# Reordering five steps of VectorE's hand-written queue in the second mixer of a ten-sublayer transformer kernel

## The chip, the core and the metric

The program runs on one NeuronCore of one Trainium2 chip. The metric is the device time of one execution in microseconds (us); lower is better. Several executions are timed and their median is given. A separate execution is profiled; its trace gives the start and the duration of every instruction.

## What is computed

One sequence of 256 tokens with 1024 features goes through ten sublayers, all in float32. Two blocks are chained: the first holds (FFN, mixer 1, FFN) twice, the second holds (mixer 2, FFN) twice and a last norm. The change touches mixer 2 alone, which therefore runs twice, as sublayers 6 and 8 (counted from 0).

```python
def mixer2(h):                            # h: normed x, 256 x 1024
    z = h @ w_in                          # split by columns
    y_a = pool_mixer(pool_u)              # running means of 2, 4, 8, 16 tokens, grouped 64x64 matmuls
    y_b = chunk_band_attention(q, k, v)   # 4 heads, relative bias
    y_c = dsa_attention(q, k, v, ...)     # 4 heads over selected keys:
    #   score = sum_h iw[h] * relu(iq[h] . ik);  keep the top 64 of every row;  softmax over those
    y_d = mla_attention(...)              # 4 heads, latent queries and keys
    y = concat([y_a, y_b, y_c, y_d])      # 4 groups of 256 features
    mix = y * rsqrt(mean(y*y per group) + eps) * g
    return x + gate * (mix @ w_out)
```

## The kernel before

**Work and staging.** Activations lie with features on the 128 partitions and tokens along the free axis. Every weight arrives by DMA in half units of 512 KB in an 8-slot ring. Exact float32 products are made from float32r parts: ScalarE copies a half unit to its high part WH (`hi_half`, `hi` for both halves of a unit), VectorE subtracts to get the low part WL (`lo_half`, `lo`), and TensorE does three matmuls for each 128x128 block. Activations are split in the same way (HH and HL, YH and YL).

**Order.** Each engine's queue is written out by hand and runs strictly in that order. Engines are tied together by counting semaphores: a producer's instruction adds one, and the consumer's queue stops until the count is reached. In mixer 2, attentions are numbered a0 to a0+5 (two MLA, two selected-key, two banded; even ones for the first 128 queries, odd ones for the last 128), and output tiles, 128 queries by 256 features, are numbered o0 to o0+7.

**Life of an output tile o.** TensorE makes it in PSUM bank 6 (`attend` or `pooled`). VectorE scales it into the buffer OT (`attended2`: a reciprocal of 4 columns and a 128x256 product; `pooled`: one 128x256 product); each adds one to `s_o`. ScalarE sums its squares and forms the RMS scale (`tile_scale`, adds one to `s_oss`). VectorE puts the scale on a diagonal matrix (`diagonal`, `s_od`). TensorE turns the tile with that diagonal into PSUM bank 7 for o0 to o0+5 (`turned_out`, `s_ot`). ScalarE copies the high part YH out of the bank (`tile_out`, `s_oh`), and VectorE subtracts to get the low part YL (`tile_rest`, two 128x128 instructions, `s_ol`), which also frees the bank for the next tile.

**Selection.** VectorE finds the 64 largest scores of a row in eight rounds of 8 (`largest(t, rounds)`, in each round MAX8 and then MATCH_REPLACE8), and then `selected(t)` turns the marks into an additive mask WKR and adds one to `s_sel`. TensorE needs that mask at the start of `sa_score`. `maxima2(a, t)` reduces an attention's scores to negated row maxima, for ScalarE's exponentials.

**TensorE's order around the change.** While the last input unit (`columns(n, 9, ...)`, CAK) is multiplied, between its two halves comes `beside_cak`. Its steps wait for VectorE like this:

```python
pooled(1, o0 + 3)             # wait_ge(s_o, o0 + 3): tiles o0, o0+1 and o0+2 scaled out of bank 6
turned_out(n, o0 + 1)         # wait_ge(s_od, o0 + 2); wait_ge(s_ol, o0 + 1): tile_rest(o0) done
attend(a0 + 2, 0, r0 + 4, o0 + 4, of_sa)  # wait_ge(s_apt, r0 + 4); wait_ge(s_o, o0 + 4): VectorE's pooled(1) done
sa_score(a0 + 3, 1)           # wait_ge(s_aex, a0 + 3); wait_ge(s_sel, 2 * l + 2): selected(1) done
turned_out(n, o0 + 2)         # wait_ge(s_od, o0 + 3); wait_ge(s_ol, o0 + 2): tile_rest(o0 + 1) done
```

**ScalarE's order there:** `tile_out(o0)`, `by_keys(r0 + 3)`, `tile_scale(o0 + 2)` (waits for `s_o` of o0+3), `hi(u0 + 10)` (the first output-weight unit), `tile_scale(o0 + 3)`, `tile_out(o0 + 1)`, `tile_scale(o0 + 4)`, `tile_out(o0 + 2)`, `exponents2(a0 + 3)`.

Of the kernel before, what the change touches and what calls it, by code (L numbers as in the profile page):

```python
# [87 lines left out]
def build(nc, A):  # L88
    ctx = ExitStack()
    with ctx:  # L90
# [89 lines left out]
        def vec(name, i=0, n=1):  # L180
            return VC[:, VEC[name] + i:VEC[name] + i + n]
# [9 lines left out]
        def v3(ap, a):  # L191
            return ap.rearrange("p (a s) -> p a s", a=a)
# [146 lines left out]
        def score_bank(n, b, t):  # L339
            w = 128 * (t + 1)  # L340
            return PS[:, b:b + t + 1, :].rearrange("p a s -> p (a s)").rearrange("p (h k) -> p h k", h=4)
# [32 lines left out]
        def summed2(n, r, c):  # L374

            k, k0 = (len(ROUNDS[SUBS[n][0]][i]) for i in (r, 0))
            last = (k0 * KD if r else 0) + k * c + k - 1
            if last % 8 == 7:
                return s_half, down_half(n) + last // 8 + 1
            return s_op2, 8 * MIX_AT[n] + 4 * r + c // 2 + 1  # L380
# [4 lines left out]
        def out_bank2(n, r, c):  # L385
            banks = out_banks(n, r)
            return PS[:, banks[c % len(banks)], 0:256]

        def turn_bank(n, o):

            o -= OUT0[n]
            return 6 + o % 2 if SUBS[n][0] == "mix1" else (7, 7, 7, 7, 7, 7, 4, 5)[o]
# [9 lines left out]
        def gains_of(n):  # L402
            return f"gmix{SUBS[n][1]}" if SUBS[n][0] == "mix1" else f"ggroup{SUBS[n][1]}"
# [1273 lines left out]
        def _(e):  # L1677
            count = {"step": 0}

            def step(ins):  # L1680

                count["step"] += 1
                ins.then_inc(s_dstep, 1)
                e.wait_ge(s_dstep, count["step"])

            def ts(out, a, s1, s2, op0, op1):
                return e.tensor_scalar(out, a, s1, s2, op0) if s2 is None else e.tensor_scalar(out, a, s1, s2, op0, op1)  # L1687

            def tt(out, a, b, op):
                return e.tensor_tensor(out, a, b, op)  # L1690

            def stt(out, a, s, b, op0, op1):
                return e.scalar_tensor_tensor(out=out, in0=a, scalar=s, in1=b, op0=op0, op1=op1)  # L1693
# [144 lines left out]
            def diagonal(n, o):  # L1838
                e.wait_ge(s_oss, o + 1)
                if o >= OUT0[n] + 2:  # L1840
                    e.wait_ge(s_ot, o - 1)
                ts(DG[o % 2], ident1, SM_[:, 114 + o % 2:115 + o % 2], None, ALU.mult, None).then_inc(s_od, 1)

            def tile_rest(n, o):
                at, t = OTILES[SUBS[n][0]][o - OUT0[n]]
                q = slice(128 * t, 128 * t + 128)
                e.wait_ge(s_oh, o + 1)
                for c in range(2):
                    last = stt(YL[:, at + c, q], PS[:, turn_bank(n, o), 256 + 128 * c:384 + 128 * c], vec(gains_of(n), at + c),
                               YH[:, at + c, q].bitcast(F32), ALU.mult, ALU.subtract)  # L1850
                last.then_inc(s_ol, 1)

            def partial(n, c):

                e.wait_ge(*summed2(n, 0, c))
                stt(X[:, c, :], out_bank2(n, 0, c), MOD[:, 24 * n + 16 + c:24 * n + 17 + c], X[:, c, :], ALU.mult,
                    ALU.add).then_inc(s_xp, 1)
# [164 lines left out]
            def mixer2(n):  # L2022
                l = SUBS[n][1]
                u0 = UNIT0[n]
                a0, r0, p0, o0 = ATT0[n], TR0[n], PROJ0[n], OUT0[n]
# [14 lines left out]
                def largest(t, rounds):  # L2040

                    m = 128 * (t + 1)
                    m8 = stat[2 + t][:, 0:8]
                    for r in rounds:
                        src = SC[t][:, 0:m] if r == 0 else WK[t][:, 0:m]
                        if r == 0:
                            e.wait_ge(s_wsum, 2 * l + t + 1)
                        step(e.max(m8, src))  # L2048
                        step(e.match_replace(WK[t][:, 0:m], m8, src, LOWEST))  # L2049

                def selected(t):
                    m = 128 * (t + 1)
                    wk = WK[t][:, 0:m]
                    step(tt(wk, wk, SC[t][:, 0:m], ALU.not_equal))
                    ts(WKR[t][:, :], wk, BIG, -BIG, ALU.mult, ALU.add).then_inc(s_sel, 1)
# [27 lines left out]
                def maxima2(a, t, scaled=False):  # L2083

                    st = stat[a % 2]
                    e.wait_ge(s_asc, a + 1)
                    ins = e.tensor_reduce(st[:, 0:4], score_bank(n, 2, t), AX.X, ALU.max, negate=True)  # L2087
                    if scaled:
                        step(ins)
                        e.wait_ge(s_rq, l + 1)  # L2090
                        ins = ts(st[:, 4:8], st[:, 0:4], rq[:, t:t + 1], None, ALU.mult, None)
                    ins.then_inc(s_amx, 1)

                def tile_free(o):

                    if o >= o0 + 4:
                        e.wait_ge(s_ot, o - 3)

                def attended2(a, o):
                    st = stat[a % 2]  # L2100
                    e.wait_ge(s_aex, a + 1)
                    step(e.reciprocal(st[:, 12:16], st[:, 8:12]))
                    e.wait_ge(s_apv, a + 1)
                    tile_free(o)
                    tt(v3(OT[o % 4], 4), v3(PS[:, 6, 0:256], 4),
                       st[:, 12:16].rearrange("p (h o) -> p h o", o=1).to_broadcast([128, 4, 64]), ALU.mult).then_inc(s_o, 1)

                def pooled(t, o):
                    e.wait_ge(s_poolmm, 2 * l + t + 1)
                    tile_free(o)  # L2110
                    tt(OT[o % 4], PS[:, 6, 0:256], PSR, ALU.mult).then_inc(s_o, 1)
# [54 lines left out]
                maxima2(a0 + 2, 0)  # L2166
                diagonal(n, o0 + 1)
                largest(1, (3, 4))
                attended2(a0 + 1, o0 + 2)
                largest(1, (5, 6, 7))  # L2170
                tile_rest(n, o0)
                pooled(1, o0 + 3)
                selected(1)
                diagonal(n, o0 + 2)
                attended2(a0 + 2, o0 + 4)
                lo_half(2 * u0 + 20)
# [13 lines left out]
                lo_half(2 * u0 + 23)  # L2190
                attended2(a0 + 3, o0 + 5)
                partial(n, 1)
                diagonal(n, o0 + 5)
                maxima2(a0 + 5, 1)
                attended2(a0 + 4, o0 + 6)
                partial(n, 2)
                share(n, 2)
# [49 lines left out]
            for n, (kind, l, _) in enumerate(SUBS):  # L2247
                if n == 1:
                    e.wait_ge(s_const_rest, 16)
                if kind == "mix1":  # L2250
                    mixer1(n)
                elif kind == "mix2":
                    mixer2(n)
                else:
                    ffn(n)
# [180 lines left out]
```

## Time and profile before

| | |
|---|---|
| time, median of 3 executions | 1614.84 us (1614.66 to 1617.54) |
| the profiled execution's own time | 1614.81 us |
| its span in the trace | 1613.0 us |
| granted TensorE clock, mean | 0.997 of 2.4 GHz |
| busy share: TensorE / VectorE / ScalarE / GpSimd | 97% / 80% / 57% / 15% |

The span runs from the first to the last instruction of the trace; the execution's time holds 1.8 us more around it. In the rows, PE is TensorE, DVE is VectorE and ACT is ScalarE. L552, L1687, L1690 and L1693 are helper lines that many steps share (`mm`, `ts`, `tt` and `stt`), so steps are told apart by tile, shape and start time. OT lies in the tensor SQ; the diagonal and the work arrays of the selection lie in SCR.

### The profile page before, as it was taken

The page shows a single profiled execution, that of the slowest core. Times are in us where ns is not written, and L with a number is a line of the kernel's source. Part 1 is how long each engine was busy: PE and PEld are TensorE (multiplying, and loading weights), DVE is VectorE, ACT ScalarE, POOL GpSimd, SP SyncE. Part 2 cuts the span into 40 slices and gives each one's busy share as a digit, 9 for nine tenths or more (in the row PEclk, how much of TensorE's full clock was granted, in tenths as well). Part 3 has the DMA queues.
Part 4 walks back from the last instruction along what each step waited for, and adds up shares of the span by engine and source line. Part 5 has one row for each costly group of instructions (what it writes and reads, how often), then busy time and mean ns, then how long its engine had stood idle before and what let it go on. Part 6 is the DMA issues. An engine that isn't in the chain of part 4 may idle for free.

```text
span 1613.0 us, 32436 instructions
## 1 busy us (share of the span) xinstructions
PE 1570.0 (97%) x13288; PEld 1549.7 (96%) x13288; DVE 1285.8 (80%) x1935; ACT 912.1 (57%) x1569; POOL 237.5 (15%) x255
## 2 busy tenths in 40 slices
PE   4999999999999999999999999999999999999998
PEld 3999998999999999998999999999999999999998
DVE  6688888788788888888688898788888878786553
ACT  5445458664555545458665445666645466664453
POOL 4122000022210122000022231001222010021100
PEclk9999999999999999999999999999999999999999
DMA  9899974559988799874459988534899873457761
GB/s 346 330 305 323 317 266 137 183 169 329 314 311 314 265 317 314 310 244 150 165 187 344 317 309 289 181 105 157 292 330 336 309 251 130 132 182 239 239 215 42
DMA packets 110996, 403.11 MB, mean 250 GB/s; under 512 B 12562, under 2 KB 12818, under 8 KB 110720
## 3 DMA queue, kind: packets, MB, share of 16 engines
q1 hardware_dynamic: 109280, 395.87, 71.2%
q0 software_dynamic: 1568, 5.17, 1.2%
q8 instruction: 105, 1.72, 0.4%
q14 instruction: 43, 0.35, 0.1%
HBM read 399.94 MB, written 1.05 MB: 249 GB/s over the span
## 4 chain that ended last, share of the span: by engine, by line
PE 86%; DVE 8%; ACT 3%; DMA 1%; issue 1%; SPq 0%; DVEq 0%; ACTq 0%
PE PS L552 85%; DVE WL L1690 2%; DVE SCR L1693 1%; DMA ring<-in_ada 1%; DVE SCR L1690 1%; ACT WH L1205 1%; DVE ring L1716 1%; DVE SCR L2049 0%; DVE SCR L1687 0%; DVE SMALL L2087 0%; ACT SCR L1495 0%; DVE SMALL L2048 0%; PE PS L1041 0%; DVE MOD L1687 0%; ACT HH L1237 0%
## 5 line engine op out<-in xcount | busy, mean ns | idle before, releaser
L1690 DVE TENSOR_TENSOR WL<-ring,WH 128x1024 fp32r<-128x1024 f32 (+1 forms) x508 | 604.2, 1224 | 191.3 <-ACT WH L1205 190.4
L552 PE MATMUL PS<-HH,WH 128*128 128x256 f32 (+1 forms) x2640 | 632.3, 281 | 3.3 <-ACT WH L1205 3.3
L552 PE MATMUL PS<-HL,WH 128*128 128x256 f32 (+1 forms) x2640 | 618.4, 278 | 0.0
L1205 ACT ACTIVATE WH<-ring 128x1024 fp32r<-128x1024 f32 (+1 forms) x508 | 511.4, 1049 | 47.6 <-PE PS L552 45.9
L552 PEld LDWEIGHTS PS<-HH,WH 128*128 128x128 f32 x2640 | 497.6, 189 | 4.4 <-ACT WH L1205 3.4
L552 PEld LDWEIGHTS PS<-HL,WH 128*128 128x128 f32 x2640 | 492.9, 189 | 0.6
L552 PE MATMUL PS<-HH,WL 128*128 128x256 f32 (+1 forms) x2640 | 378.0, 279 | 2.5 <-DVE WL L1690 2.3
L552 PEld LDWEIGHTS PS<-HH,WL 128*128 128x128 f32 x2640 | 338.7, 189 | 3.7 <-DVE WL L1690 3.7
L1716 DVE CUSTOM_DVE_ANT_0 ring<-ring,CB,VC 128x1024 f32<-128x1024 f32 x238 | 330.7, 1407 | 11.5 <-DMA ring<-in_ada 11.4
L552 PE MATMUL PS<-AH,WL 128*128 128x256 f32 x1056 | 293.0, 277 | 1.1 <-DVE WL L1690 1.1
L552 PE MATMUL PS<-AH,WH 128*128 128x256 f32 x1056 | 293.2, 278 | 0.0
L552 PE MATMUL PS<-AL,WH 128*128 128x256 f32 x1056 | 292.8, 277 | 0.0
L516 POOL TENSOR_TENSOR AL<-SCR,AH 128x256 fp32r<-128x256 f32 x132 | 152.7, 1159 | 595.8 <-ACT AH L1263 595.8
L552 PEld LDWEIGHTS PS<-AH,WL 128*128 128x128 f32 x1056 | 198.3, 188 | 1.3 <-DVE WL L1690 1.3
L552 PEld LDWEIGHTS PS<-AL,WH 128*128 128x128 f32 x1056 | 199.1, 189 | 0.0
L552 PEld LDWEIGHTS PS<-AH,WH 128*128 128x128 f32 x1056 | 198.3, 188 | 0.0
L1263 ACT ACTIVATE AH<-SCR 128x256 fp32r<-128x256 f32 x132 | 55.2, 419 | 226.1 <-DVE SCR L1690 220.2
L476 POOL TENSOR_TENSOR SQ<-SQ 128x256 f32<-128x256 f32 x54 | 46.2, 855 | 585.3 <-ACT SQ L1221 584.1
L1218 ACT ACTIVATE HH<-X,AB 128x256 fp32r<-128x256 f32 x72 | 36.6, 508 | 117.9 <-DVE X L1693 117.4
L1290 ACT ACTIVATE SCR<-PS 128x256 f32<-128x256 f32 x122 | 46.4, 380 | 89.8 <-PE PS L552 89.8
L552 PE MATMUL PS<-SCR 128*128 128x64 f32 (+4 forms) x528 | 87.0, 310 | 2.3 <-ACT SCR L1360 1.7
L1693 DVE SCALAR_TENSOR_TENSOR X<-PS,MOD,X 128x256 f32<-128x256 f32 x112 | 53.3, 478 | 37.1 <-PE PS L552 36.7
(214 smaller groups left out, 1480.7 us busy)
## 6 DMA issues: line engine op xcount, KB each, us to landing
ring<-in_up SPq DMA_DIRECT2D x176, 512.0 KB, 5.6
ring<-in_ada SPq DMA_DIRECT2D x144, 512.0 KB, 6.0
ring<-in_ffn SPq DMA_DIRECT2D x132, 512.0 KB, 4.8
ring<-in_mod SPq DMA_DIRECT2D x96, 512.0 KB, 5.8
ring<-in_down SPq DMA_DIRECT2D x88, 512.0 KB, 5.6
ring<-in_win SPq DMA_DIRECT2D x64, 512.0 KB, 5.4
ring<-in_wout SPq DMA_DIRECT2D x32, 512.0 KB, 4.7
ring<-in_winv SPq DMA_DIRECT2D x8, 512.0 KB, 4.5
```

The source lines that it names most:

```text
L476: e.tensor_tensor(SQ[:, c, :], SQ[:, c - 1, :], SQ[:, c, :], ALU.add).then_inc(s_psum, 1)
L516: e.tensor_tensor(AL[:, f, :], G6[:, 3 + f % 3, :], AH[:, f, :].bitcast(F32), ALU.subtract).then_inc(s_al, 1)
L552: return e.matmul(out, lhsT, rhs, start=start, stop=stop, skip_group_check=skip)
L1205: e.activation(half_of(i)[0], slot_of(("half", i, 0))[:, 0:w], ACT.Copy).then_inc(s_hi, 1)
L1218: e.activation(HH[:, c, 0:S], X[:, c, :], ACT.Copy, scale=AB[:, 8 * m + c:8 * m + c + 1]).then_inc(s_yh, 1)
L1263: e.activation(AH[:, f, :], G6[:, 3 + f % 3, :], ACT.Copy).then_inc(s_ah, 1)
L1290: e.activation(G6[:, f % 3, :], PS[:, up_bank(f), 0:256], ACT.Silu).then_inc(s_silu, 1)
L1690: return e.tensor_tensor(out, a, b, op)
L1693: return e.scalar_tensor_tensor(out=out, in0=a, scalar=s, in1=b, op0=op0, op1=op1)
L1716: ins = e.tensor_tensor_reduce(out=w, in0=w, in1=CB[:, :], scale=1.0, scalar=bias, op0=ALU.mult, op1=ALU.add, accum_out=MOD[:, 2 * i + j:2 ...
```

## The change

In VectorE's queue of `mixer2` alone, three moves; no instruction is added, removed or resized. `tile_rest(n, o0)` goes ahead of the selection's last three rounds instead of behind them. `attended2(a0 + 1, o0 + 2)` goes from ahead of those rounds to behind them and behind `selected(1)`; `pooled(1, o0 + 3)` thereby comes behind `selected(1)` too. Further down, `maxima2(a0 + 5, 1)` goes ahead of `diagonal(n, o0 + 5)`.

```diff
                 diagonal(n, o0 + 1)
                 largest(1, (3, 4))
+                tile_rest(n, o0)
+                largest(1, (5, 6, 7))
+                selected(1)
                 attended2(a0 + 1, o0 + 2)
-                largest(1, (5, 6, 7))
-                tile_rest(n, o0)
                 pooled(1, o0 + 3)
-                selected(1)
                 diagonal(n, o0 + 2)
                 attended2(a0 + 2, o0 + 4)
                 lo_half(2 * u0 + 20)
@@
                 attended2(a0 + 3, o0 + 5)
                 partial(n, 1)
+                maxima2(a0 + 5, 1)
                 diagonal(n, o0 + 5)
-                maxima2(a0 + 5, 1)
                 attended2(a0 + 4, o0 + 6)
                 partial(n, 2)
```

## Rows read from the trace of the kernel before

**Rows 1.** The page: busy time by engine, and shares of the chain that ended last.

```profile
PE 1570.0 (97%) x13288; PEld 1549.7 (96%) x13288; DVE 1285.8 (80%) x1935; ACT 912.1 (57%) x1569; POOL 237.5 (15%) x255
...
PE 86%; DVE 8%; ACT 3%; DMA 1%; issue 1%; SPq 0%; DVEq 0%; ACTq 0%
```

**Rows 2.** Waits of TensorE, whole span: total us, times, longest.

```profile
PE PS L552 <- DVE YL L1693: 1.8, 2, 0.9
PE PS L1041 <- ACT SCR L1495: 1.1, 2, 0.6
```

**Rows 3.** Timeline of TensorE, sublayer 6: start, us, operation, [idle before <- releaser].

```profile
1068.88 1.07 PE L552 MATMUL PS<-HH,WL 128*128 128x256 f32 x8
1069.79 0.60 PE L552 MATMUL PS<-SCR 128*128 128x128 f32 x4
1071.29 0.68 PE L552 MATMUL PS<-SCR,SQ 128*128 128x128 f32 x4 [0.90 <-DVE YL L1693]
1071.81 1.00 PE L552 MATMUL PS<-SCR 128*128 128x64 f32 x8
1072.62 0.70 PE L552 MATMUL PS<-WKR,identr 128*128 128x512 f32 x2
...
1076.67 0.61 PE L552 MATMUL PS<-SCR,SQ 128*128 128x128 f32 x4
```

**Rows 4.** Timeline of VectorE, the same stretch.

```profile
1067.03 0.18 DVE L2102 RECIPROCAL SMALL<-SMALL 128x4 f32<-128x4 f32 x1
1067.25 0.42 DVE L1690 TENSOR_TENSOR SQ<-PS,SMALL 128x256 f32<-128x256 f32 x1
1067.59 0.42 DVE L2048 MAX8 SMALL<-SCR 128x8 f32<-128x256 f32 x1
...
1070.54 0.61 DVE L1693 SCALAR_TENSOR_TENSOR YL<-PS,VC,YH 128x128 fp32r<-128x128 f32 x2
1071.06 0.41 DVE L1690 TENSOR_TENSOR SQ<-PS,SCR 128x256 f32<-128x256 f32 x1
1071.39 0.41 DVE L1690 TENSOR_TENSOR SCR<-SCR 128x256 f32<-128x256 f32 x1
...
1072.05 0.28 DVE L1687 TENSOR_SCALAR SCR<-identr,SMALL 128x128 f32<-128x128 f32 x1
...
1076.87 1.23 DVE L2087 TENSOR_REDUCE SMALL<-PS 128x4 f32<-128x1024 f32 x1 [1.69 <-PE PS L552]
```

**Rows 5.** Timeline of ScalarE, the same stretch.

```profile
1066.86 0.64 ACT L1323 ACTIVATE YH<-PS,VC 128x128 fp32r<-128x128 f32 x2
...
1067.84 0.46 ACT L1315 ACTIVATE SCR<-SQ 128x256 f32<-128x256 f32 x1
...
1068.86 1.99 ACT L1205 ACTIVATE WH<-ring 128x1024 fp32r<-128x1024 f32 x2
```

**Rows 6.** Timelines of TensorE (one row) and VectorE around the third move, sublayer 6.

```profile
1091.39 0.61 PE L552 MATMUL PS<-CN,SCR 128*128 128x128 f32 x4
...
1091.66 0.29 DVE L1687 TENSOR_SCALAR SCR<-identr,SMALL 128x128 f32<-128x128 f32 x1 [0.75 <-ACT SMALL L1317]
1092.03 1.23 DVE L2087 TENSOR_REDUCE SMALL<-PS 128x4 f32<-128x1024 f32 x1
...
1094.30 0.42 DVE L1690 TENSOR_TENSOR SQ<-PS,SMALL 128x256 f32<-128x256 f32 x1 [0.96 <-DVE SMALL L2102]
```

**Rows 7.** Timeline of TensorE, the same place in sublayer 8.

```profile
1374.81 0.68 PE L552 MATMUL PS<-SCR,SQ 128*128 128x128 f32 x4 [0.89 <-DVE YL L1693]
```

**Rows 8.** Windows: PE, PEld, DVE, ACT, POOL busy, PEclk, DMA share, GB/s.

```profile
1117.00:1600.00 483.00, 481.14 (x4133) 477.61 (x4132) 365.28 (x562) 269.45 (x476) 63.97 (x67) 1.00 0.68 227
```

**Rows 9.** Windows with a lower clock, and TensorE's timeline there, at the start.

```profile
32.00:33.00 1.00, 0.00 (x0) 0.00 (x0) 1.00 (x4) 0.63 (x3) 0.00 (x0) 0.77 1.01 389
...
39.00:40.00 1.00, 1.00 (x9) 1.00 (x9) 1.00 (x2) 1.00 (x1) 0.00 (x0) 0.82 0.97 320
...
34.73 2.08 PE L552 MATMUL PS<-HH,WH 128*128 128x256 f32 x8 [3.32 <-ACT WH L1205]
```

## The prediction

> **What bounds the kernel now.** I read the page first. TensorE is busy for 97% of the span and carries 86% of the chain that ended last [rows 1], so the end moves only when TensorE's queue gains or loses idle time. Next I read the list of what TensorE waited for. In both runs of mixer 2 together it holds 1.8 us on the low part YL, 0.9 us in each, and 1.1 us on ScalarE's exponentials [rows 2]. Little is there to win: if both disappeared the kernel would gain 2.9 us, under 0.2%, and 0.2% (3.23 us) is about what a measurement of this kernel can tell from no change. Last I laid the timelines of TensorE, VectorE and ScalarE side by side around that 0.9 us wait.
>
> There the reader should see this. TensorE does the four matmuls of `pooled(1)` at 1069.79, without a wait. Then `turned_out(o0 + 1)` needs the bank that `tile_rest(o0)` frees, and starts at 1071.29 after 0.90 us idle. `attend(a0 + 2)` follows at 1071.81 and `sa_score` at 1072.62 [rows 3]. VectorE has by then been running without a gap: the reciprocal and product of tile o0+2 at 1067.03, three rounds from 1067.59 to 1070.54, the rest of tile o0 to 1071.06, the pooled product to 1071.39, the mask to 1072.05 [rows 4]. It is the limit for 1.5 us here. The order in this stretch decides which of its results TensorE gets first.
>
> **The change part by part.** No instruction is added or removed and no DMA is issued by a moved step; only VectorE's order differs. All costs come from the profiled execution (span 1613.0 us, its own time 1614.81 us, which is 0.03 us under the median).
>
> *First move, the rest of tile o0 ahead of rounds 5 to 7.* It needs YH from ScalarE, two copies that start at 1066.86 and take 0.64, so end at 1067.50 [rows 5]. The two rounds ahead of it end by 1067.03 [rows 4]; VectorE therefore sits idle for 0.50 us and starts the rest at about 1067.53. It takes 1071.06 − 1070.54 = 0.52, to 1068.05. TensorE's wait of 0.90 us on it is gone by itself: the bank is free before TensorE reaches it at about 1070.4 (1069.79 + 0.60 [rows 3]).
>
> *Second move, the attended product behind the selection.* The three rounds take 1070.54 − 1067.59 = 2.95, to 1071.00. The mask takes 1072.05 − 1071.39 = 0.66, to 1071.66. The reciprocal starts there, the product 0.22 later (1067.25 − 1067.03) and needs 0.42, so tile o0+2 is out of bank 6 at 1072.30; before it was at 1067.67 [rows 4].
>
> Who waits for that? TensorE's `pooled(1)` does: it writes bank 6 and waits for `s_o` to show tile o0+2. Before, that wait was long fulfilled; now it is not. From VectorE's end to TensorE's start pass 0.14 us (YL ends at 1070.54 + 0.61 = 1071.15, TensorE starts at 1071.29) [rows 3, 4]. So `pooled(1)` starts at 1072.44 in place of 1069.79: idle time of about 2.5 us in TensorE. Everything in TensorE's queue stands behind it, although `turned_out(o0 + 1)` and `sa_score` would be ready.
>
> A second, small wait follows. The pooled matmuls take 0.68 from idle (the duration of the like group of four that starts after a wait [rows 3]; the other end is 0.60, that of the group without a wait), to 1073.12. VectorE picks that up 0.02 to 0.03 later (scores end at 1091.39 + 0.61 = 1092.00, the reduction starts at 1092.03 [rows 6]) and needs 0.41 for the pooled product, to 1073.55. The turning of tile o0+1, 0.52 long, fills part of this. `attend(a0 + 2)` starts at 1073.55 + 0.14 = 1073.69, in place of 1071.81. TensorE is **1.88 us later**; with 0.60 for the group it would be 1.80.
>
> Behind it, is more late than TensorE itself? ScalarE's `tile_scale(o0 + 2)` waits for the same tile and moves from 1067.84 to 1072.34. It and the queue behind it take: scale 1.02 (1067.84 to 1068.86), two weight copies 1.99 at most [rows 5], the next scale about 1.0, the two YH copies of tile o0+1 0.64, which ends at 1077.0. VectorE's rest of tile o0+1 then ends by 1077.6. TensorE wants it for `turned_out(o0 + 2)` at 1076.67 + 1.88 = 1078.55 [rows 3], with 0.14 for the signal: about 0.8 us to spare. The low part of output half 20 is delayed by ScalarE's copies to about 1076.3, but its first matmuls come only after the second half of CAK, which stands behind that `turned_out(o0 + 2)` at 1078.55. The SyncE loads that this slot releases move by no more than TensorE does. The row maxima of a0+3 waited 1.69 us for TensorE at 1076.87 [rows 4], so they and what follows are set by TensorE and shift with it. The cover of VectorE's and ScalarE's lateness is thus the 4 us of `sa_score`; with that gone, each would have come straight onto TensorE's path.
>
> *Third move, maxima of a0+5 ahead of the diagonal of o0+5.* The diagonal starts at 1091.66 and takes 0.29, to 1091.95; the scores that the maxima need end at 1092.00 and the reduction starts at 1092.03 [rows 6]. It gains 0.03 at most, and I take nothing. The diagonal goes behind the reduction, where the attended product that comes next waits until 1094.30 for TensorE anyway, 0.96 us of it idle [rows 6], more than the 0.2 that it is pushed. If the scores ended earlier, the gain would be up to 0.37 for each mixer (1092.03 − 1091.66); the loss is bounded by 0.29.
>
> *Sum.* Sublayer 8 shows the same wait, 0.89 us [rows 7], so two times 1.88 = 3.76 us. From 1117 to 1600 us TensorE is busy for 481.1 of 483 us at full clock [rows 8]; nothing there could give time back. 1614.81 + 3.76 = **1618.6 us**, or 0.23% slower.
>
> **The clock.** The new wait is the longest that TensorE would have after the start. At the start the trace shows what a wait of 3.32 us can do: the granted clock falls within 32 to 33 us and is back within 39 to 40 us. The two shares, 0.77 and 0.82, give 0.46 + 6 + 0.36 = 6.8 us at the lower level of 1.2 GHz, and eight matmuls take 2.08 us there against 1.07 [rows 3, 9]. That would be up to 3.4 us for each mixer. The present 0.9 us waits leave it at full level. The wait of 2.5 us lies between, nearer to the long one, but it is shorter, and dense matmuls stand on both sides; only few and small matmuls stood ahead of the long one. I take no fall as the likelier.
> The Trainium skill ("TensorE: Matmul & The Clock Gate", section "What's actually happening") says that the low clock is the default and activity releases it, so idle time may bring it back; the trace agrees for its one long wait, and no row before shows 2.5 us. By that rule acting in both mixers the sum would be up to 1625.
>
> **The rivals.**
> - *The clock falls too* (chance 0.10): as worked out, 1.7 to 3.4 us more for each mixer in which it falls; 1620.3 with one short fall, 1625.4 with two long ones. For it: the start of the trace. Against: the shorter wait, between dense matmuls.
> - *ScalarE becomes the next wait* (0.08): `tile_scale(o0 + 2)` and the two weight copies push YH of tile o0+1 past 1078.4, and `turned_out(o0 + 2)` waits. With 0.5 us for each mixer, 1619.6. Against: 0.8 us to spare.
> - *Later waits absorb some* (0.10): the 0.57 us or so on the exponentials [rows 2] shrinks if its chain is tied to loads and not to TensorE; 3.76 − 1.1 = 2.6 gives 1617.4, no change by the bound. Against: its maxima start when TensorE's scores end [rows 6].
> - *The other side, the removed wait is all that counts* (0.04): if `attended2` still ended before 1069.65 (0.14 ahead of 1069.79), `pooled(1)` would not be held, 0.90 + 0.89 us would go, and the time would be 1613.0, not slower. That asks for VectorE to be 2.65 us earlier than the sum of its rows, or for TensorE to reach `pooled(1)` that much later.
>
> **How the numbers follow.** The forecast as worked out has 0.68, with its own range of 1617.6 to 1619.5: 1.80 to 1.88 for each mixer, up to 0.37 of gain for the third move, and the scatter of the runs. Its centre is only 0.5 us above the bound of 1618.07, so about a fifth of it falls within 0.2%. Slower by over 0.2%: 0.8 × 0.68 + 0.10 + 0.08 = 0.72. Faster by over 0.2% would need 3.2 us where all waits of mixer 2 together are 2.9: 0.02. The rest, 0.26, is within. The range 1616.8 to 1621.0 takes in the absorbed case, the ScalarE case and one short fall of the clock, and leaves out long falls and the other side.
>
> **What would show it.** Right: an idle of about 2.5 us ahead of the four `pooled(1)` matmuls, released by VectorE's SQ product, in both mixers; no wait on YL; a second wait of 0.2 us or less ahead of `attend(a0 + 2)`; VectorE idle for 0.5 us on YH; the maxima of a0+5 starting with the end of the scores as before; everything from `sa_score` on later by 1.9, and after the second mixer by 3.8. Wrong: no wait at `pooled(1)`, a granted clock under 1.00 in either mixer, or new TensorE waits in the output rounds.

## The result, and the profile after

The change makes the kernel slower: ratio to the kernel before 1.0043, 95% interval 1.0025 to 1.0060, which is +4 to +10 us with the middle at +6.9. Medians are 1616.89 us after (12 executions) and 1610.06 before (12). The prediction said 1618.6, from the 1614.84 then known, so +3.8 and slower.

One thing is needed to read these medians: executions of every kernel here, the one before too, lie at two levels some 7 us apart, and the kernel before was profiled at the upper one and the kernel after at the lower. The gap is away from the change, in the first 360 us: from 340 to 360 us TensorE does 172 matmuls before and 178 after, from 360 to 380 us 179 in both. Windows of the kernel before and then of the kernel after, columns as in [rows 8], show it:

```profile
100.00:200.00 100.00, 100.00 (x851) 100.00 (x850) 82.27 (x107) 49.10 (x72) 16.94 (x15) 1.00 0.91 317
1400.00:1500.00 100.00, 100.00 (x872) 99.73 (x871) 72.31 (x114) 59.69 (x103) 18.05 (x19) 1.00 0.67 213
```

```profile
100.00:200.00 100.00, 100.00 (x885) 100.00 (x884) 84.90 (x112) 51.02 (x75) 17.67 (x16) 1.00 0.92 324
1400.00:1500.00 100.00, 100.00 (x871) 99.73 (x870) 72.86 (x116) 59.71 (x106) 18.07 (x19) 1.00 0.65 211
```

Both have the full granted clock, yet 851 matmuls against 885 in the same 100 us. Late in the kernel the counts agree. In all fourteen profiled executions of this study the first window holds 851 or 852 matmuls, or 884 or 885. So absolute times of two traces must not be subtracted from each other; a stretch between two marks inside mixer 2 can be. Sorted by level, by eye, the medians are 1609.1 and 1616.5 us before and 1615.4 and 1623.5 after: about 6.3 and 7 us slower. Below, **the stretch** is the time from the start of the last WL group ahead of `beside_cak` to the start of `turned_out(o0 + 2)`. Before it is 1076.67 − 1068.88 = 7.79 us [rows 3], and the same in sublayer 8.

TensorE's waits over the whole span of the kernel after (total us, times, longest), where [rows 2] stood before:

```profile
PE PS L552 <- DVE SQ L1690: 5.6, 5, 2.6
PE PS L1041 <- ACT SCR L1495: 1.1, 2, 0.6
```

The wait on YL is gone, and a longer one on VectorE's scaled tile is there. Its five times are 2.58 us in each mixer, 0.16 in sublayer 8, and two of 0.15 to 0.2 us ahead of an earlier step, which the kernel before has too. The wait on the exponentials is as it was. TensorE's timeline in sublayer 6, the counterpart of [rows 3]:

```profile
1062.50 1.07 PE L552 MATMUL PS<-HH,WL 128*128 128x256 f32 x8
1066.15 0.86 PE L552 MATMUL PS<-SCR 128*128 128x128 f32 x4 [2.58 <-DVE SQ L1690]
1066.80 1.06 PE L552 MATMUL PS<-SCR,SQ 128*128 128x128 f32 x4
1067.65 1.90 PE L552 MATMUL PS<-SCR 128*128 128x64 f32 x8
1069.31 1.20 PE L552 MATMUL PS<-WKR,identr 128*128 128x512 f32 x2
...
1075.30 0.61 PE L552 MATMUL PS<-SCR,SQ 128*128 128x128 f32 x4
```

and the same place in sublayer 8, the counterpart of [rows 7]:

```profile
1371.07 1.07 PE L552 MATMUL PS<-HH,WL 128*128 128x256 f32 x8
...
1374.71 0.68 PE L552 MATMUL PS<-SCR 128*128 128x128 f32 x4 [2.58 <-DVE SQ L1690]
...
1376.00 1.08 PE L552 MATMUL PS<-SCR 128*128 128x64 f32 x8 [0.16 <-DVE SQ L1690]
1376.89 0.71 PE L552 MATMUL PS<-WKR,identr 128*128 128x512 f32 x2
...
1380.95 0.61 PE L552 MATMUL PS<-SCR,SQ 128*128 128x128 f32 x4
```

The reader should compare the durations. The wait is 2.58 us in both. But in sublayer 6 the eight matmuls of `attend` then take 1.90 us where sublayer 8 has 1.08, and the first two of `sa_score` 1.20 against 0.71. The stretch is 12.80 us in sublayer 6 and 9.88 in sublayer 8, so 5.01 and 2.09 longer than before, 7.10 us together. That is the whole loss: from the start of the stretch in sublayer 6 to the end of the span, where the early levels play no part, pass 1613.0 − 1068.88 = 544.1 us before and 1613.8 − 1062.50 = 551.3 after, 7.2 more. The windows say why the two sublayers differ (the seventh group of numbers, PEclk, is the granted clock):

```profile
1066.00:1067.00 1.00, 0.85 (x5) 0.89 (x6) 0.00 (x0) 0.90 (x4) 0.00 (x0) 0.76 0.00 0
1067.00:1073.00 6.00, 6.00 (x24) 5.43 (x23) 2.97 (x8) 4.30 (x13) 0.00 (x0) 0.50 0.13 40
1073.00:1074.00 1.00, 1.00 (x8) 0.95 (x7) 0.00 (x0) 0.00 (x0) 0.00 (x0) 0.83 0.75 303
...
1374.00:1382.00 8.00, 7.13 (x52) 6.70 (x53) 4.45 (x12) 5.61 (x18) 0.00 (x0) 1.00 0.23 67
```

After the wait in sublayer 6 the granted clock is 0.50, 1.2 GHz, for 0.48 + 6 + 0.34 = 6.8 us. In sublayer 8 it stays at 2.4 GHz. VectorE's timeline shows the cause of the wait, the counterpart of [rows 4]:

```profile
1061.23 0.61 DVE L1693 SCALAR_TENSOR_TENSOR YL<-PS,VC,YH 128x128 fp32r<-128x128 f32 x2 [0.61 <-ACT YH L1323]
1061.76 0.42 DVE L2048 MAX8 SMALL<-SCR 128x8 f32<-128x256 f32 x1
...
1065.16 0.29 DVE L1687 TENSOR_SCALAR WKR<-SCR 128x256 fp32r<-128x256 f32 x1
1065.37 0.17 DVE L2102 RECIPROCAL SMALL<-SMALL 128x4 f32<-128x4 f32 x1
1065.58 0.42 DVE L1690 TENSOR_TENSOR SQ<-PS,SMALL 128x256 f32<-128x256 f32 x1
1067.04 0.42 DVE L1690 TENSOR_TENSOR SQ<-PS,SCR 128x256 f32<-128x256 f32 x1 [1.04 <-PE PS L552]
```

VectorE idles for 0.61 us on YH, then does the rounds and the mask, and tile o0+2 leaves bank 6 at 1066.00; TensorE starts 0.15 later. At the third move, the counterpart of [rows 6], the maxima start when TensorE's scores end, as before:

```profile
1090.67 1.23 DVE L2087 TENSOR_REDUCE SMALL<-PS 128x4 f32<-128x1024 f32 x1 [1.12 <-PE PS L552]
1091.81 0.28 DVE L1687 TENSOR_SCALAR SCR<-identr,SMALL 128x128 f32<-128x128 f32 x1
...
1092.94 0.42 DVE L1690 TENSOR_TENSOR SQ<-PS,SMALL 128x256 f32<-128x256 f32 x1 [0.76 <-DVE SMALL L2102]
```

### The profile page after: what moved, and what is told of

It is laid out like the page before. It is cut to its first block, busy times and chain, and to the rows that moved or that the text cites. A ratio compares the mean times of both kernels' runs of the same rounds, so it can differ in the third digit from the quotient of the medians.

```text
span 1613.8 us, 32434 instructions
## 1 busy us (share of the span) xinstructions
PE 1567.4 (97%) x13288; PEld 1546.1 (96%) x13288; DVE 1285.1 (80%) x1935; ACT 912.1 (57%) x1569; POOL 237.7 (15%) x255
## 4 chain that ended last, share of the span: by engine, by line
PE 85%; DVE 8%; ACT 3%; DMA 1%; issue 1%; SPq 0%; DVEq 0%; ACTq 0%
PE PS L552 85%; DVE WL L1690 2%; DMA ring<-in_ada 1%; DVE SCR L1693 1%; DVE SCR L1690 1%; ACT WH L1205 1%; DVE ring L1716 1%; ACT SCR L1495 1%; DVE SMALL L2087 0%; DVE SCR L1687 0%; DVE SCR L2049 0%; PE PS L1041 0%; DVE MOD L1687 0%; DVE SMALL L2048 0%; DVE SQ L1690 0%
## 5 line engine op out<-in xcount | busy, mean ns | idle before, releaser
L1690 DVE TENSOR_TENSOR WL<-ring,WH 128x1024 fp32r<-128x1024 f32 (+1 forms) x508 | 604.0, 1223 | 187.0 <-ACT WH L1205 186.7
L552 PEld LDWEIGHTS PS<-SCR 128*128 128x128 f32 (+1 forms) x528 | 75.8, 194 | 13.8 <-issue 8.6
```

The costliest lines, as they stand in the source:

```text
L552: return e.matmul(out, lhsT, rhs, start=start, stop=stop, skip_group_check=skip)
```

## The experiments

"Before" is the kernel before, timed again beside each run on its chip. Theory A: the second move alone does the harm, by a wait of 2.6 us that costs 2.1, and a lost clock that costs about as much again where it occurs. Theory B: the wait is the whole loss. All diffs are in VectorE's queue of mixer 2 unless said otherwise.

**The changed kernel again, twice.** No edit.

> The changed kernel once more. Theory A (the wait plus the clock): TensorE idle for 2.6 us ahead of the pooled(1) matmuls in both mixers, 2.1 us lost in each, and in some of these places the granted clock falls to half for some 7 us, which costs 3.1 us more each time; against before +4.2 us without a fall, +7.3 with one, +10.4 with two. Theory B (the wait alone is the whole loss, and the fall that the first profile shows is an exception): +4.2 us and no fall in either mixer. In both theories no other new TensorE wait.

Measured: ratio 1.0062 (1.0041 to 1.0083). Both waits ahead of `pooled(1)` are there (2.58 and 2.56 us), and the stretches are 11.51 and 13.08 us: the clock fell in both mixers. The other repetition:

> The changed kernel a third time, on the chip of the run with four extra matmuls. Both theories: idle 2.6 us ahead of pooled(1) in both mixers. Theory A: each place costs 2.1 us without a fall and 3.7 to 5.3 with one; the mean granted clock of a run is lower than before by 0.002 for each fall, and runs show 1 or 2 falls: +7 to +10 us against before. Theory B: +4.2 us.

Measured: 1.0042 (1.0023 to 1.0061), stretches 13.15 and 12.63 us, again a fall in both. So over three profiled executions the clock fell in five places of six, for 1.6 to 3.3 us each beyond the 2.09 of the wait. The falls have two lengths. The one in sublayer 6 of the first repetition is short:

```profile
1067.00:1068.00 1.00, 0.84 (x8) 0.68 (x7) 0.70 (x3) 0.97 (x3) 0.00 (x0) 1.00 0.06 16
1068.00:1071.00 3.00, 3.00 (x12) 2.63 (x12) 1.62 (x3) 2.94 (x10) 0.00 (x0) 0.50 0.00 0
1071.00:1072.00 1.00, 1.00 (x7) 0.97 (x6) 0.65 (x3) 0.59 (x4) 0.00 (x0) 0.79 0.14 29
```

It is 3 + 0.42 = 3.4 us at half clock and costs 1.6 us; the other four last 6.8 us and cost 2.8 to 3.3. The mean granted clock over all timed executions agrees: 0.9948 for the change (28 executions) against 0.9975 before (84). That difference is 0.0027 × 1613 / 0.5 = 8.7 us at half clock for each execution, where the three profiled ones have 10.2. At the price of those (13.8 us lost in 30.7 us at half clock) it costs 3.9 us, and with 2 × 2.09 for the waits the loss would be 8.1 us, an estimate; three measurements gave 6.9, 10.0 and 6.8. Theory B is out.

**The wait filled with work.** From the changed kernel, on TensorE, at the head of `beside_cak`; the half bank that is written is overwritten by the next half unit. A second kernel has `range(4)` in its place.

```diff
                 def beside_cak():
+                    for _ in range(8):
+                        mm(PS[:, 1, 256:512], ones, const("cos"))
                     pooled(1, o0 + 3)
```

> The changed kernel with eight extra 128x256 float32 matmuls of constants at the head of beside_cak, into the half of PSUM bank 1 that the next half unit overwrites; they take about 1.8 us, which ends before VectorE's product of tile o0+2 does, so they fill the wait and move nothing. Theory A: the remaining wait is 0.8 us, the granted clock stays at 1.00 in both mixers, and the time is that of the wait alone, +4.2 us against before, 3 us or more faster than the changed kernel where that one loses its clock. Theory B: the same time as the changed kernel. Third possibility (the extra matmuls themselves lengthen the path): slower than the changed kernel.

Measured with eight: 1.0062 (1.0039 to 1.0085). The extra work took 3.45 us, twice what I had reckoned, since each such matmul makes two records of 0.22 us. That is longer than the wait, and the stretch became 10.51 and 10.50 us. The clock was 1.00 throughout. The medians can't be compared, since 4 of the 6 executions lie at the upper level and 1 of 6 of the repetition on the same chip; level by level this kernel is 4.2 and 3.6 us faster than the repetition, from few executions. To keep the extra work inside the wait, four:

> The changed kernel with four extra matmuls in place of eight. The eight of the filled wait took 3.45 us and not 1.8, longer than the wait itself; four take 1.7 us and end inside it. Theory A (wait plus clock): a rest of 0.8 to 0.9 us of idle ahead of pooled(1), granted clock 1.00 in both mixers, the stretch from the last WL group of CAK's first half to the first output matmul 14.4 us in both (before 12.3; the changed kernel 14.4 without a fall and 16.0 to 17.6 with one); against before +4.2 us, 2 to 5 us faster than the changed kernel on the same chip. Theory B (the wait is all): the same time as the changed kernel.

Measured: stretches 9.89 us in both mixers, granted clock 1.00 in both. TensorE's timeline in sublayer 6, and then the windows around the place in both mixers (the two new lines of source make L1690 into L1692):

```profile
1062.23 1.07 PE L552 MATMUL PS<-HH,WL 128*128 128x256 f32 x8
1063.14 1.89 PE L552 MATMUL PS<-CN 128*128 128x256 f32 x8
1065.88 0.68 PE L552 MATMUL PS<-SCR 128*128 128x128 f32 x4 [0.85 <-DVE SQ L1692]
1066.40 0.61 PE L552 MATMUL PS<-SCR,SQ 128*128 128x128 f32 x4
1067.17 1.08 PE L552 MATMUL PS<-SCR 128*128 128x64 f32 x8 [0.16 <-DVE SQ L1692]
```

```profile
1062.00:1075.00 13.00, 11.99 (x87) 11.00 (x86) 9.23 (x24) 7.25 (x25) 0.00 (x0) 1.00 0.12 42
...
1367.00:1380.00 13.00, 11.99 (x88) 10.99 (x87) 9.20 (x24) 6.61 (x21) 0.00 (x0) 1.00 0.14 41
```

`pooled(1)` starts 3.65 us after the WL group, exactly as in the changed kernel, so the wait for VectorE is untouched; only idle time was replaced by useless work, and the clock stayed. The mean clock over its 11 executions is 0.9975, that of the kernel before. Its ratio, 1.0044 (1.0026 to 1.0062), shows no gain over the repetition on the same chip (1.0042). But 6 of its 11 executions lie at the upper level, against 2 of 10 (one at 1615.3 us, between the levels, is counted as lower). Level by level its medians are 1612.4 and 1620.1 against 1616.2 and 1625.4, so 3.8 and 5.4 us faster than the change; against before (1609.0 and 1615.6) it is 3.4 and 4.5 slower, where 4.2 was expected. Its trace says the same without levels: 1610.6 − 1062.23 = 548.4 us from the stretch's start to the end of the span, 4.3 more than before. The two parts are separated: about 4.2 us for the waits, 3 to 5 for the clock.

**The first and third moves without the second.** The edit is against the changed kernel.

```diff
                 largest(1, (3, 4))
+                attended2(a0 + 1, o0 + 2)
                 tile_rest(n, o0)
                 largest(1, (5, 6, 7))
-                selected(1)
-                attended2(a0 + 1, o0 + 2)
                 pooled(1, o0 + 3)
+                selected(1)
```

> The first and third moves without the second: attended product of tile o0+2, rest of tile o0, rounds 5 to 7, pooled product, mask. Theory A: the loss comes from the second move alone. The wait on YL goes, but VectorE's pooled product comes no earlier (1071.47 in the times of before), so TensorE waits some 0.85 us for that one instead, ahead of attend(a0+2); the gain is 0.2 us for each mixer, 0.4 in all, -0.4 us against before, not to be told from no change; no fall of the clock. Rival (the removed wait counts in full): -1.8 us. Rival (the early rest does the harm, because VectorE idles on YH): +1 us or more.

Measured: 1.0007 (0.9992 to 1.0021), no change; stretches 7.69 and 7.68 us, 0.1 shorter than before. The wait of 0.90 on YL became this one:

```profile
1072.71 0.61 PE L552 MATMUL PS<-SCR,SQ 128*128 128x128 f32 x4
1074.10 1.08 PE L552 MATMUL PS<-SCR 128*128 128x64 f32 x8 [0.78 <-DVE SQ L1690]
```

The turning goes at once, and the next step waits in its place, for VectorE's pooled product. The rest ahead of the rounds is harmless and worth a tenth.

**The second move alone, on the kernel before.**

```diff
                 largest(1, (3, 4))
-                attended2(a0 + 1, o0 + 2)
                 largest(1, (5, 6, 7))
                 tile_rest(n, o0)
-                pooled(1, o0 + 3)
                 selected(1)
+                attended2(a0 + 1, o0 + 2)
+                pooled(1, o0 + 3)
```

> The kernel before with the second move alone: rounds 5 to 7, rest of tile o0, mask, attended product of tile o0+2, pooled product. Theory A: nothing idles on YH, so the attended product ends 0.5 us sooner than in the changed kernel; TensorE waits 2.0 to 2.1 us ahead of pooled(1) and loses 1.4 us in each mixer, +2.8 us against before, and +6 if the clock falls in one of them. Rival (the first move is the harmful one): no change against before.

Measured: 1.0034 (1.0018 to 1.0050); waits of 1.99 and 2.00 us, stretches 9.29 us (+1.50, no fall) and 10.94 (a fall). The second move alone makes the kernel slower; the first adds the time that VectorE idles on YH.

**The attended product one step earlier, then two.** Both start from the changed kernel. The first edit puts the product between `largest(1, (5, 6, 7))` and `selected(1)`, the second, shown here, between rounds 6 and 7:

```diff
                 tile_rest(n, o0)
-                largest(1, (5, 6, 7))
+                largest(1, (5, 6))
+                attended2(a0 + 1, o0 + 2)
+                largest(1, (7,))
                 selected(1)
-                attended2(a0 + 1, o0 + 2)
```

> The changed kernel with the attended product of tile o0+2 behind round 7 but ahead of the mask. Theory A: TensorE's wait ahead of pooled(1) is shorter by the mask's 0.66 us, so 1.9 us, and a second wait of 0.1 to 0.2 us stands ahead of attend(a0+2), 1.4 to 1.5 us lost in each mixer: +2.9 us against before without a fall of the clock. If a wait of 1.9 us is too short for a fall, both mixers show 1.00; if not, +6. Rival (the order against the mask does not matter): the same as the changed kernel.

Measured: 1.0056 (1.0038 to 1.0075). Waits of 1.91 us in both mixers; stretches 9.22 us (+1.43) and 12.44 (a fall). A single wait of 1.91 us is enough for a fall, not each time. The medians differ by more than the 6 us expected, but 3 of the 6 executions lie at the upper level, against 2 of 17 before.

> The changed kernel with the attended product of tile o0+2 between rounds 6 and 7. Theory A: two waits in place of one long: about 1.0 us ahead of pooled(1) and again about 1.0 ahead of attend(a0+2), since VectorE's pooled product still comes behind the mask; 1.1 to 1.3 us lost in each mixer, +2.3 us against before, and no fall of the clock, since each wait is short. Rival (the sum of the idle time counts, not the single wait): a fall here too, as idle time in this stretch is again 2 us.

Measured: 1.0028 (1.0011 to 1.0046). Stretches 10.54 and 8.92 us. Here my expectation failed in its second half, as TensorE's timeline and then the windows of sublayer 6 show:

```profile
1070.86 0.68 PE L552 MATMUL PS<-SCR 128*128 128x128 f32 x4 [0.92 <-DVE SQ L1690]
1071.38 0.61 PE L552 MATMUL PS<-SCR,SQ 128*128 128x128 f32 x4
1072.84 1.55 PE L552 MATMUL PS<-SCR 128*128 128x64 f32 x8 [0.84 <-DVE SQ L1690]
```

```profile
1070.00:1073.00 3.00, 1.29 (x10) 1.16 (x10) 2.80 (x11) 2.19 (x6) 0.00 (x0) 1.00 0.00 0
1073.00:1079.00 6.00, 6.00 (x31) 5.47 (x31) 2.27 (x5) 3.02 (x11) 0.00 (x0) 0.72 0.27 90
```

No wait is longer than 0.92 us, which is what the kernel before has without any fall, and yet the clock falls: TensorE was busy for only 1.29 of these 3 us. Here two short waits close together did what one long one does. In sublayer 8, with the same two waits (0.93 and 0.84), it did not fall, so this rests on one place of two.

**The third move alone, on the kernel before.**

```diff
+                maxima2(a0 + 5, 1)
                 diagonal(n, o0 + 5)
-                maxima2(a0 + 5, 1)
```

> The kernel before with the third move alone (the maxima of a0+5 ahead of the diagonal of o0+5). Theory A: nothing, at most 0.03 us for each mixer, since the reduction starts when TensorE's scores end and not when the diagonal does: 0.0 us, all waits of TensorE as before. Rival: up to 0.37 us gained or 0.29 lost for each mixer, so -0.7 to +0.6 us.

Measured: 1.0016 (0.9997 to 1.0036), no difference that can be told; stretches 7.80 and 7.80 us. TensorE's waits in mixer 2 are those of before, 1.8 us on YL and 1.1 on the exponentials.

**A version for the better.** VectorE is what is late here, and one of its steps is not needed yet: the second half of `lo(u0 + 9)`, 1.2 us, which TensorE uses only after `sa_score`. The full edit on the changed kernel, and below it the simple one on the kernel before:

```diff
-                lo(u0 + 9)
+                lo_half(2 * u0 + 18)
...
                 largest(1, (3, 4))
+                attended2(a0 + 1, o0 + 2)
+                largest(1, (5,))
                 tile_rest(n, o0)
-                largest(1, (5, 6, 7))
-                selected(1)
-                attended2(a0 + 1, o0 + 2)
+                largest(1, (6, 7))
                 pooled(1, o0 + 3)
+                selected(1)
+                lo_half(2 * u0 + 19)
                 diagonal(n, o0 + 2)
```

```diff
-                lo(u0 + 9)
+                lo_half(2 * u0 + 18)
...
                 selected(1)
+                lo_half(2 * u0 + 19)
                 diagonal(n, o0 + 2)
```

> A version meant to beat both: from the changed kernel, the second half of lo(u0+9) goes behind the mask (TensorE needs it last of these), the attended product of tile o0+2 goes back ahead of round 5, the rest of tile o0 between rounds 5 and 6, the pooled product behind round 7, then the mask. Theory A (VectorE's 1.17 us of weight remainder is what makes it late here): the mask is done 0.6 us sooner, TensorE's waits in this stretch shrink from 0.9 to about 0.1 to 0.3 us, sa_score starts 0.8 us earlier in each mixer: -1.7 us against before, 6 to 8 us faster than the change. Rival: the ring slot that comes free 8 us later delays two loads, and VectorE waits for one of them after sa_score: then no gain, or a loss of about 1 us.

Measured: 0.9988 (0.9972 to 1.0003), stretches 7.18 and 7.17 us. Repeated on another chip, beside the simple edit:

> The version with the weight remainder behind the mask and the rest of tile o0 between rounds 5 and 6, once more, beside its simpler relative. Measured first at 0.9988 of before with an interval that just holds 1. Theory A: -1.3 to -1.7 us, stretch to the first output matmul 0.5 to 0.8 us shorter than before in each mixer, no fall of the clock. Rival: no gain, the first result was scatter.

> The kernel before with one edit: the second half of lo(u0+9) behind the mask. Theory A: VectorE has 1.17 us less ahead of the mask, so the rest of tile o0 is done before TensorE asks, the wait on YL (0.9 us) goes and one of 0.1 to 0.2 us on the pooled product stays: sa_score starts 0.7 to 0.85 us earlier in each mixer, -1.6 us against before, as much as the version that also moves the rest of tile o0. Rival (the early rest is needed too): -0.4 us or less.

Measured: the full edit 0.9994 (0.9976 to 1.0012), stretches 7.18 and 7.18 us; the simple one 1.0006 (0.9988 to 1.0025), 7.11 and 7.11. In the simple one no wait at all is left in the stretch:

```profile
1069.58 1.10 PE L552 MATMUL PS<-HH,WL 128*128 128x256 f32 x8
1070.53 0.60 PE L552 MATMUL PS<-SCR 128*128 128x128 f32 x4
1071.07 0.68 PE L552 MATMUL PS<-SCR,SQ 128*128 128x128 f32 x4
1071.74 1.07 PE L552 MATMUL PS<-SCR 128*128 128x64 f32 x8
1072.63 0.72 PE L552 MATMUL PS<-WKR,identr 128*128 128x512 f32 x2
```

The stretches show 0.68 us gained in each mixer, 1.4 us in all, and the early rest of tile o0 is not needed for it. The timing can't tell that from no change: 7 of the 12 executions of the simple edit lie at the upper level, against 8 of 32 of the kernel before. The full edit is clearly better than the change (its two intervals end at 1.0003 and 1.0012, those of the change begin at 1.0023 and above). That either beats the kernel before is shown for the stretch; for the whole time it is likely but not shown. Level by level the medians of these three runs lie 1.0 to 3.0 us below those of the kernel before on their chips, and from the stretch's start to the end of the span their traces have 0.5, 1.4 and 1.5 us less than its 544.1.

## Why the prediction was right, and where it was short

- *The bound, and the waits before*: right. TensorE's queue sets the end, and what its stretch lost is what the kernel lost. One small slip: the waits of mixer 2 before are 3.3 us and not 2.9, since two of 0.2 us on VectorE's scaled tile (0.4 in all) were left out; nothing in the sum hangs on it.
- *First move*: right. The wait on YL is gone, VectorE idles on YH for 0.61 us where 0.50 was said, and alone the move is worth 0.1 us.
- *Second move*: right in place, cause and partner wait: `pooled(1)` held by `s_o` (2.58 us of idle where "about 2.5" was said), and 0.16 us again ahead of `attend`. The term of 1.88 us for each mixer measured 2.09. Of the 0.21, 0.09 is the later YH and pick-up, 0.04 lies between `pooled(1)` and `attend`, and 0.08 is `attend` itself after a wait (0.89 to the next step, before 0.81).
- *ScalarE and VectorE behind it*: right. No new wait on YH, YL or WL came; outside a fall, the time from the start of `sa_score` to `turned_out(o0 + 2)` is 4.06 us, as before (4.05).
- *Third move*: right, nothing.
- *The clock*: this step failed, and the prediction's own sign of being wrong, "a granted clock under 1.00 in either mixer", was seen. The prediction held the clock's fall for a rival at 0.10 with the words "I take no fall as the likelier". It fell in five places of six, which took the loss from the 3.76 of the sum to 6.9 us. The price was right (1.7 to 3.4 us said, 1.6 to 3.3 measured); the likelihood was not. The ground "dense matmuls stand on both sides" did not hold: behind the wait come only small groups with a second wait of 0.16 us among them, and the dense ones ahead did not prevent a fall. The 0.9 us waits of before are harmless singly, but another such wait 1.1 us behind the first sufficed for a fall in one place of two.

The Trainium skill ("TensorE: Matmul & The Clock Gate", section "What's actually happening") says that the low clock is the default and activity releases it. The traces agree: each fall came behind idle time of TensorE, and each ended, after 3.4 or 6.8 us, while it was working.

The time of 1616.9 lies in the range of 1616.8 to 1621.0 by luck, only because the kernel before came out 4.8 us under the median known then and the loss 3.1 us over the sum; the two errors offset each other. What the study leaves open: what decides whether a given wait makes the clock fall, and for 3.4 or for 6.8 us (waits of 1.9 to 2.6 us did in seven places of ten, counting all kernels with idle waits of that size), and what sets the two levels of the first 360 us.

## What to carry to other kernels

Before an engine's step is moved back, look for the queue that counts its semaphore, even where that wait is invisible in the trace of before because it was always fulfilled: here a PSUM bank that had to be emptied cost 2.1 us where the removed wait had cost 0.9. Removing a wait of an engine that waits for one late partner gains only what the next result of that partner allows; take work off the late engine instead (a weight remainder that nobody needs yet). On TensorE, add the clock to the price of a new wait: here one of 1.9 to 2.6 us brought a fall in seven places of ten and two of 0.9 us close together in one of two, and each fall cost another 1.6 to 3.3 us.

## What the runs showed of the hardware

- The granted clock fell to one half behind 1.9 to 2.6 us of idle that followed dense matmuls, and once behind two waits of 0.92 and 0.84 us that lay 1.1 us apart. It stayed down for 3.4 us in three places (1.6 us lost in each) and for 6.8 us in five (2.8 to 3.3 us lost). The fall began between 0.3 us before TensorE's restart after the long wait and 2.0 us after it. The same wait in the same kernel did and did not bring a fall (sublayers 6 and 8 of the first profile).
- Filling 1.7 of the 2.6 us with matmuls whose result nobody reads kept the clock at 1.00 in both mixers, and the mean of 11 executions is that of the kernel before (0.9975).
- At a granted clock of 1.00 TensorE can still do 4% fewer matmuls in one execution than in another of the same kernel (851 or 885 in the 100 us from 100 to 200 us), which no column of the windows explains.
